# Two-block transformer kernel: the modulation's sums in the RWKV scan go from VectorE to ScalarE and GpSimd

## What is computed

```python
mod = jax.nn.silu(c) @ ada_w + ada_b
sh_m, sc_m, g_m, sh_f, sc_f, g_f = jnp.split((mod + ada_table[layer])[:, None, :], N_MOD, axis=-1)
h = _rms(x, norm_mix_pre[layer]) * (1 + sc_m) + sh_m
y, v_first = _rwkv7_mix(h, v_first, ...)          # 32 heads of 64, a recurrence over 256 steps
x = x + g_m * _rms(y, norm_mix_post[layer])
h = _rms(x, norm_ffn_pre[layer]) * (1 + sc_f) + sh_f
f = _conv_ffn(h, ...)
x = x + g_f * _rms(f, norm_ffn_post[layer])
```

## Time and profile before

| | |
|---|---|
| median of 3 runs | 2868.64 us (2866.64 to 2879.68) |
| the profiled execution | 2867.14 us, its span 2865.3 us |
| busy over the span | PE 94%, DVE 65%, ACT 46%, POOL 6% |
| share of the chain that ended last | PE 81%, DVE 8%, ACT 6% |

### The profile page before, as it was taken

One profiled execution on the slowest core, in us unless ns is written; L12 is line 12 of the kernel. 1 busy time (PEld: TensorE's weight loads), 2 busy tenths in 40 slices (PEclk: granted clock), 3 DMA queues, 4 the chain that ended last, 5 costly groups with the idle time before them and its releaser, 6 DMA issues.

```text
span 2865.3 us, 57084 instructions
## 1 busy us (share of the span) xinstructions
PE 2694.4 (94%) x25250; PEld 2540.4 (89%) x25250; DVE 1869.7 (65%) x2436; ACT 1312.1 (46%) x1768; POOL 177.8 (6%) x167
## 2 busy tenths in 40 slices
PE   6899997889889899999999989999999999999997
PEld 2489995767769799999999989999989999999997
DVE  3787656777755766767867666567657556566665
ACT  1244434353434655345445555456555444343443
POOL 0121002111001000000000021000020000000001
PEclk9999997998989999999999999999999999999999
DMA  9767652222326365866676544543355565665662
GB/s 374 277 223 241 233 188 77 96 99 96 108 103 204 104 200 178 281 201 200 245 251 195 184 155 154 176 147 103 121 160 165 203 192 188 198 195 191 184 205 90
DMA packets 289255, 514.84 MB, mean 180 GB/s; under 512 B 10096, under 2 KB 122736, under 8 KB 288880
## 3 DMA queue, kind: packets, MB, share of 16 engines
q1 hardware_dynamic: 286016, 500.21, 52.3%
q0 software_dynamic: 2560, 7.90, 0.8%
q10 hardware_dynamic: 432, 3.07, 0.3%
HBM read 508.91 MB, written 2.10 MB: 178 GB/s over the span
## 4 chain that ended last, share of the span: by engine, by line
PE 81%; DVE 8%; ACT 6%; issue 3%; DMA 2%; POOL 0%; DVEq 0%; SPq 0%; ACTq 0%
PE ps L806 45%; PE ps L814 22%; ACT WHb L1246 2%; DMA RAWa<-in_ada_w 2%; PE ps L955 2%; PE ps L715 1%; PE ps L950 1%; PE ps L775 1%; PE ps L940 1%; DVE WLb L1777 1%; PE ps L745 1%; PE ps L1102 1%; PE ps L907 1%; PE ps L1006 1%; DVE ACCs L1760 1%
## 5 line engine op out<-in xcount | busy, mean ns | idle before, releaser
L806 PE MATMUL ps<-XB,WHb 128*128 128x256 f32 x4608 | 642.0, 281 | 29.3 <-issue 11.0
L806 PEld LDWEIGHTS ps<-XB,WHb 128*128 128x128 f32 x4608 | 578.4, 190 | 39.0 <-issue 19.6
L1777 DVE TENSOR_TENSOR WLb<-RAWb,WHb 128x2048 fp32r<-128x2048 f32 (+1 forms) x196 | 426.4, 2191 | 251.4 <-ACT WHb L1246 251.4
L1777 DVE TENSOR_TENSOR WLd<-RAWd,WHd 128x2048 fp32r<-128x2048 f32 x144 | 328.3, 2290 | 252.7 <-ACT WHd L1246 252.7
L1246 ACT ACTIVATE WHb<-RAWb 128x2048 fp32r<-128x2048 f32 (+1 forms) x196 | 358.3, 1840 | 290.8 <-PE ps L814 248.8
L1246 ACT ACTIVATE WHd<-RAWd 128x2048 fp32r<-128x2048 f32 x144 | 274.3, 1916 | 330.4 <-PE ps L814 330.4
L814 PE MATMUL ps<-XB,WLb 128*128 128x256 f32 x2304 | 360.3, 278 | 0.0
L806 PE MATMUL ps<-XD,WHd 128*128 128x256 f32 x2560 | 349.2, 279 | 8.7 <-issue 6.1
L806 PEld LDWEIGHTS ps<-XD,WHd 128*128 128x128 f32 x2560 | 317.9, 189 | 11.2 <-issue 6.4
L814 PEld LDWEIGHTS ps<-XB,WLb 128*128 128x128 f32 x2304 | 308.2, 189 | 0.0
L806 PE MATMUL ps<-FB,WHd 128*128 128x256 f32 x2048 | 275.9, 277 | 1.1 <-DVE R L1833 0.9
(11 more groups left out here) (334 smaller groups left out, 3468.2 us busy)
## 6 DMA issues: line engine op xcount, KB each, us to landing
RAWb<-in_ffn_w_in SPq DMA_DIRECT2D x168, 512.0 KB, 5.0
RAWd<-in_w_up SPq DMA_DIRECT2D x64, 1024.0 KB, 5.6
RAWd<-in_w_down SPq DMA_DIRECT2D x64, 1024.0 KB, 5.1
RAWa<-in_ada_w SPq DMA_DIRECT2D x48, 1024.0 KB, 7.3
RAWa<-in_rwkv_w_rkv SPq DMA_DIRECT2D x48, 1024.0 KB, 5.4
RAWb<-in_ffn_w_out SPq DMA_DIRECT2D x36, 1024.0 KB, 5.6
RAWs<-in_ada_w SPq DMA_DIRECT2D x32, 1024.0 KB, 5.0
RAWb<-in_w_in SPq DMA_DIRECT2D x44, 512.0 KB, 4.9
```

The costliest lines, as they stand in the source:

```text
L806: pe.matmul(banks[tile_bank[i]][:, z:z + T], WH[tag][:, w, o:o + P], acts(k)[:, z:z + T], start=(k == 0 and half == 0), stop=False, skip_g ...
L1777: dve.tensor_tensor(WL[tag][:, n % WN, 0:size], RAW[tag][:, slot, 0:size], WH[tag][:, n % WN, 0:size].bitcast(F32), ALU.subtract).then_inc ...
```

## The change

DVE's `ada_round` goes. Each half is now two instructions. ACT scales it in place in the ring (`ada_scale`, L1452 of the changed kernel) and raises a new semaphore `s_adsc`; POOL adds it to `ACCs` (`ada_add`, L2460; the first of a piece is a copy, L2463) and raises `s_ada`. PE, SP and the counts of `s_ada` stay as they are. POOL's `side` gets three yields, so that the first adds stand between its parts, and the first memset waits for the first chunk's second add, the third add for the second memset.

```diff
+            def ada_scale(r):
+                for m in range(4):
+                    i = end_r + 4 * r + m
+                    for k in range(2):
+                        src = RAW["s"][:, slot_of[i], k * 1024:(k + 1) * 1024]
+                        j = 2 * stream[i]["kc"] + k
+                        act.wait_ge(*landed[i])
+                        act.activation(src, src, ACT.Copy, scale=SC[:, j:j + 1]).then_inc(s_adsc, 1)
+                        yield
+                        yield
...
             for r in range(10):
-                weave(stage_s(r - 1) if 0 < r < 9 else None, side(r), first_weights() if r == 8 else None)
+                weave(stage_s(r - 1) if 0 < r < 9 else None, side(r),
+                      ada_scale(r) if r < 8 else first_weights() if r == 8 else None)
...
-            def ada_round(r):
-                yield
-                for m in range(4):
-                    for k in range(2):
-                        ada_half(end_r + 4 * r + m, k)
-                        yield
-                        if m + k < 4:
-                            yield
...
+            def ada_add(r):
+                for m in range(4):
+                    i = end_r + 4 * r + m
+                    piece, kc = stream[i]["piece"], stream[i]["kc"]
+                    acc = acc_of("s", piece)
+                    for k in range(2):
+                        src = RAW["s"][:, slot_of[i], k * 1024:(k + 1) * 1024]
+                        pool.wait_ge(s_adsc, 8 * r + 2 * m + k + 1)
+                        if (m, k) == (1, 0) and r < 7:
+                            pool.wait_ge(*aG(r + 1, "zu"))
+                        pool.wait_ge(s_ada, ada_half_no(stream[i]["number"], k) - 1)
+                        if 2 * kc + k:
+                            pool.tensor_tensor(acc, src, acc, ALU.add).then_inc(s_ada, 1)
+                        else:
+                            pool.wait_ge(s_adamm, piece - 1)
+                            pool.tensor_copy(acc, src).then_inc(s_ada, 1)
+                        yield
...
-            for r in range(-1, 10):
-                side(r)
+            weave(side(-1))
+            for r in range(10):
+                weave(side(r), ada_add(r) if r < 8 else None)
```

More of the change, by code:

```diff
@@ L227, in two_blocks @@
         s_ada, s_adamm, s_mod = sem("ada"), sem("adamm"), sem("mod")
+        s_adsc = sem("adsc")
         s_bar = sem("bar")
@@ L2316, in vector_program @@
                 weave(stage_t(r) if r < 8 else None, stage_s(r - 1) if 0 < r < 9 else None, side(r),
-                      ada_round(r) if r < 8 else first_weights() if r == 8 else None)
+                      first_weights() if r == 8 else None)
             barrier(dve, tally)
@@ L2460, in side @@
                     pool.wait_ge(*aG(b, "ka"))
+                    if r >= 0:
+                        pool.wait_ge(s_ada, ada_half_no(stream[end_r + 4 * r]["number"], 1))
                     pool.memset(UV[64:128, :, 0, :], 0.0).then_inc(aG.sem, 1)
```

## The result

| | before | after |
|---|---|---|
| median, the runs timed together | 2870.75 us | 2922.54 us (2914.46 to 2933.54) |
| ratio, 95% interval | | 1.0163 [1.0130, 1.0196] |
| the profiled execution, its span | 2867.14, 2865.3 us | 2914.46, 2912.6 us |
| busy over the span | PE 94%, DVE 65%, ACT 46%, POOL 6% | PE 93%, DVE 63%, ACT 47%, POOL 11% |
| the scan, from the product ahead of round 0 to the memset of `UT` | 422.3 us | 459.7 us |

2895 was forecast, with a range to 2914. The direction was right, the size too small.

A forecast was written before the change was run, and what follows sets the result against it. The scan was taken as a relay between PE, DVE and ACT, no engine full. Terms -10.9 + 12.4 + 17.7 + 4.7 + 2.1 = +26.0 us gave 2895 us; forecast case 2880 to 2905, chance 0.55, range 2862 to 2914.

The forecast's parts named there:

- the halves gone from DVE: Scan, rounds 0 to 7: removing DVE's 64 halves of 1.28 us shortens the chain where DVE stands on it, -10.9 us.
- scales at the round end and in round 8: Two ACT scales of 2.08 us behind MX at five round ends, 10.4 us; two ahead of RST in round 8, +1.1.
- scales of the first chunk: ACT scales ahead of a table load and Ln in round 0 and the copy of RST in round 1: 0.9 + 1.05 us.
- lock: Rounds 0 to 6: POOL's adds hold off DVE's AR, BK and MX, two operands in SBUF, delaying WS: +17.7 us.
- ties: Rounds 0, 1, 3, 5: third add and DVE's next instruction ready within 0.1 us; half of them counted, +4.7 us.
- the ring in round 7: Round 7's first chunk waits for round 6's sixth add, so its scale stands late ahead of RST: +1.0 us.
- the other adds, priced at nothing: Adds behind the wait for L917 meet mostly DVE instructions on PSUM, so no lock cost was counted.
- and 5 us for PE: Upper end of the forecast, 2905: all ties, 2900, plus 5 us for a granted clock lower if PE waits more.
- In later rounds two PE operations cover it: After round 1, the first chunk's scale ahead of RST is covered by two PE operations; no cost counted.
- the rival on GpSimd: Adds of 3.5 us make POOL the bound and chunks land late, some 2.5 us a round, six rounds: 2910 us, chance 0.13.

The follow-up runs named there:

- e_none: Changed kernel with every scale and add of the scan on 8 columns, instructions, waits and semaphores kept: scan 418.2 us, ratio 0.9969 against before.
- e_busy_end: Changed kernel plus six useless 256-column matmuls on PE ahead of each round's first product: scan 450.0 us, ratio 1.0106 against before.
- e_gone: Kernel before with DVE's halves, but a piece's first, replaced by 8-column memsets, nothing added on ACT or POOL: scan 412.7 us, ratio 0.9960.
- e_end_only: Changed kernel with all adds and scales on 8 columns except the scales of each round's fourth chunk: scan 431.2 us, ratio 1.0045 against before.
- e_scales_only: Changed kernel with all scales whole and every add on 8 columns: scan 440.7 us, ratio 1.0053 against before.
- e_boundary: Changed kernel with only the scales of each round's fourth chunk on 8 columns: scan 443.8 us, ratio 1.0082 against before.
- e_early: Changed kernel with only the scales of each round's first chunk on 8 columns: scan 460.7 us, ratio 1.0151 against before.
- e_again: Changed kernel run once more, unedited: scan 460.6 us, ratio 1.0144 against before (medians 2914.73 and 2877.34 us).
- e_control: Kernel before run once more, unedited, with a second profile: scan 422.6 us, ratio 0.9988 against before.

## Why the prediction was half right

The predicted sum and the measured steps of the scan. Each step is measured on top of the ones above it, but for the first chunk's scales, which were added to e_none:

| step | predicted | measured |
|---|---|---|
| the halves gone from DVE | -10.9 | -9.6 |
| the new instructions, waits and order, empty | 0 | +5.5 |
| scales at the round end and in round 8 | 10.4 + 1.1 | +13.0 |
| scales of the first chunk | 1.95 | +1.9 |
| all scales together, beyond these | 0 | +7.6 |
| the adds (lock and ties; the ring in round 7) | 22.4 + 1.0 | +19.0 |
| sum | +26.0 | +37.4 |

**Right: the removal.** The 16.5 us of DVE on the chain were read place by place down to 10.9, and 9.6 came.

**Right: the round end.** Two scales between `MX` and the next round's first instruction, on the chain, five times. Alone they cost 13.0 for the 11.5 said, of which PE's wait at the five ends makes 8.4 for 10.4. A scale takes 1.14 us (1132 to 1164 ns) and not the 1.04 of the copy in the earlier trace rows.

**Right in kind: the lock.** `AR` and `BK` at 1.65 and 2.83 us in round 3, `WS` 5.5 us behind `AR`. An add takes 2.36 us (2343 to 2889 ns) for the 2.33 forecast. In size the term was wrong: the adds beside `AR`, `BK` and `MX` make PE wait some 13 us longer for `WS`, not 22.4, and taking them out gives back 9.7. That all adds together cost 19.0 is near the 22.4 by luck, for the other adds, priced at nothing, cost 9.3.

**Wrong: the step "and 5 us for PE".** The forecast put PE's clock at nought in the sum and gave it 5 us at the end of the range, with the granted clock of rounds 3 and 4 as its only row. The scan's own row shows 12.7 us more of PE's busy time for the same matmuls, and e_busy_end gets 9.7 us of the length back by filling nothing but the wait at the round end. In size that is the missing 11.4 us of the scan (37.4 less 26.0). The terms that I left at nought or too small are those where it shows: 4.0 of the 5.5 us of e_none over e_gone are PE's busy time (near that column's spread of 3), 5.0 of the 9.5 from e_end_only to e_scales_only, and 7.7 of the 19.0 from there to the changed kernel. The round ends' waits alone cost only 1.8 us of busy time (e_end_only), in company 8.8 (e_boundary).

**Wrong: that the terms add.** Each wait was priced as if the rest of the round went on at the old pace. All scales cost 7.6 us more than those of the end and of the first chunk apart, the adds 2.6 more beside the scales than alone (19.0 and 16.4). PE's busy time shows part of it, as above; how the waits work together on the clock, the runs don't show.

**Wrong: "In later rounds two PE operations cover it"**, of the scale ahead of `RST`. PE's wait for `RST` is 4.2 us in e_none, 7.7 with the first chunk's scales, 9.4 with all. What that does to the length is small, 1.9 us alone and nothing in e_early.

**A part of the rival on GpSimd came true in one place.** From round 6 to 7 the chain runs through three adds, a load of 5.07 us and a scale, and PE waits 2.56 us for `RST` (L991 at 810.74). In the other rounds POOL keeps up, as was said.

**What stays open.** The time's ratio gives 37 to 56 us in the first set of runs and 33 to 50 in the second; the scan accounts for 38. With the scan's 37.4 alone the kernel would have taken some 2906 us, inside the range of the forecast; the other 14 of the first comparison's 52 have no place in any profile and did not come again in e_again (37.4 us between the medians). Whether the change costs a few us behind the scan can't be told, since that part differs by 11.5 us between executions of one kernel. The 5.5 us of the empty instructions weren't taken apart, nor was the busy time that the adds cost outside the lock on `AR`, `BK` and `MX`.

## What to carry to other kernels

Where TensorE sets the end, price a new wait twice: by its length, and by what its clock may do to the work behind it; look for rows that get slower behind a wait, and take the loss from a stretch at either level. Before a low stretch of one profile is made the reason for anything, look at the same place in a second profile of the same kernel. Moving elementwise work with two SBUF operands from VectorE to GpSimd does not free VectorE where it works on SBUF as well: here 80 us of removed work left it 40 us less busy. And before moving work to another engine, try moving it within its own: a later place in the same queue, together with filled waits of TensorE, made the scan 6.6 us shorter where the transfer made it 37 longer; the later place alone gave nothing.

## What the runs showed of the hardware beyond what I expected

Filling a wait of 2.9 us with six matmuls of 0.46 us held the granted clock at 1.00 at the end of round 3, where it fell to 0.50 without them, and five such fillings made the scan 9.7 us shorter; eight and ten of them in twelve waits made it 4.5 us longer. Two executions of one kernel differ in where the clock is low: in round 4 the kernel before is back at 1.00 from 654 on, the same kernel in e_control is at 0.50 until 656, and their scans are 0.3 us apart. An instruction of 8 columns with two SBUF operands takes 1.23 us beside a GpSimd product, against 0.21 us for the same one at 572.77. Two memsets of 128 x 1024 on GpSimd in place of an add leave `BK` and `MX` on VectorE at 683 and 688 ns.
